# Twelve gate panels of a token mixer, given other places in TensorE's order

## The chip, the cores and the metric

The kernel runs on one core of a Trainium2 chip. The metric is the device time of one execution in microseconds (us).

## The reference, cut to what matters

Two transformer blocks on 256 tokens of width 1024, in float32. The change touches the token mixer, which is in each of the two layers of the first block:

```
proj = h @ w_in;  (a, q, k, v, qi, ki, wi, hq, hf, hi, hg, gates) = split(proj)
y_a = pool_mixer(a);  y_b = sparse_attention(q, k, v, qi, ki, wi)      # 2 blocks of 128 queries
y_c = hgrn2(hq, hf, hi, hg)                                            # gated recurrence, then
                                                                       # o * rsqrt(mean(o*o)) per head
g = sigmoid(gates.reshape(B, S, 3, D_MODEL))
merged = g[0]*(y_a @ w_branch[0]) + g[1]*(y_b @ w_branch[1]) + g[2]*(y_c @ w_branch[2])
return merged @ w_out
```

`gates` is h times 3072 columns of weights. It depends on nothing but h, and it is wanted only when the branches are merged. In attention, index scores (8 heads, ReLU, weighted sum) choose 64 keys for each query; the softmax is taken over those.

## The kernel before, in words

Weights come as panels of 1024 x 256 (1 MB) through four slots in SBUF. SP issues their DMAs in one fixed order, and waits before each until the panel four places earlier has been used. Products land in four accumulator banks `accs` that rotate in the same way; four more PSUM banks, `mix`, belong to the small products of the mixer. Each engine runs its own list, written out by hand, and waits on semaphores. All activations have tokens in the free dimension: H[:, k, lat] is 128 features by 256 tokens.

The mixer of a layer has these stages, and after each TensorE, ScalarE and VectorE wait for one another (`stage_end`): 15 input panels; pooling; attention; the recurrence; branch products (4 panels, 12 accumulators, multiplied by the gates on VectorE); output (4 panels). The 12 panels of `gates` are put between the rest: `gate(l, u)` in TensorE's list is one panel of 16 matmuls, `gate(l, u)` in ScalarE's list copies its accumulator to `gates`. Panels 0 and 1 are in pooling, 2 to 5 in attention, 6 to 11 in the recurrence.

Attention: TensorE makes the index scores of query block 0 and of block 1, then the logits of both (L812); ScalarE takes the ReLU of the scores; VectorE sums them and finds the 64 largest in 8 rounds, block 0 first, then block 1 (each round a Max8 and a MatchReplace), adds mask and bias to the logits and takes the maximum; ScalarE takes Exp; VectorE divides; TensorE transposes (L821), ScalarE copies, TensorE multiplies with v (L829), and ScalarE copies the output.

Recurrence (hgrn): 256 tokens are one tree of 8 levels. At level lv ScalarE takes the Exp of two sums, VectorE adds up the sums of the next level, multiplies (x) and takes the products of the level before out of `mix` (L1912, a copy under a mask). TensorE's products for i = 0 to 8 (L850, L853) need x of level i-1; ScalarE's Exp of level lv waits for the products i = lv-1, which read the buffer that it overwrites. Then come the output products (L861 to L863), their squares on ScalarE, mean squares over a head (L867) on TensorE, square root on ScalarE, reciprocal on VectorE, `spread` (L760, which turns the column into rows) on TensorE, and VectorE's last product. Before these, ScalarE takes the Sigmoid of all of `gates` at once.

Of the kernel before, what the change touches and what calls it, by code (L numbers as in the profile page):

```python
# [215 lines left out]
def program(nc, io):  # L216
    G, order, finished, _ = plan()
    w8, w11, wc = io["w8"], io["w11"], io["wc"]
    with ExitStack() as ctx:
# [372 lines left out]
        def _(pe):  # L592
# [203 lines left out]
            def attention(l):  # L796
                for qb in range(2):
                    n = P * (qb + 1)
                    for b in range(4):
                        if qb == 1:  # L800
                            pe.wait_ge(S("idx_relu"), 8 * l + b + 1)
                        for i in range(2):
                            r = slice(64 * (b // 2), 64 * (b // 2) + 64)
                            mm = pe.matmul(mix[:, b, i * T:i * T + n], qiT[r, 2 * (b % 2) + i, qb * P:qb * P + P], kiT[r, 0:n],
                                           start=True, stop=True)
                        mm.then_inc(S("idx_mm"), 1)
                for qb in range(2):
                    n = P * (qb + 1)
                    pe.wait_ge(S("idx_relu"), 8 * l + 4 + 2 * qb + 2)
                    for h in range(4):  # L810
                        r = slice(64 * (h % 2), 64 * (h % 2) + 64)
                        mm = pe.matmul(mix[:, 2 * qb + h % 2, h // 2 * T:h // 2 * T + n],  # L812
                                       qT[r, h // 2, qb * P:qb * P + P], kT[r, h // 2, 0:n], start=True, stop=True)
                    mm.then_inc(S("logit_mm"), 1)
                gate(l, 2, 3, 4, 5)
                for qb in range(2):
                    pe.wait_ge(S("prob_ready"), 2 * l + qb + 1)
                    for h in range(4):
                        for s in range(qb + 1):
                            i = h * (qb + 1) + s  # L820
                            mm = pe.transpose(mix[:, 2 * qb + i // 4, i % 4 * P:i % 4 * P + P],  # L821
                                              logit[:, qb, h, s * P:s * P + P], ident)
                    mm.then_inc(S("probT_mm"), 1)
                for qb in range(2):
                    pe.wait_ge(S("probT_ready"), 2 * l + qb + 1)
                    for i in range(4):
                        h = 2 * (i % 2) + i // 2
                        for s in range(qb + 1):
                            mm = pe.matmul(mix[64 * (h % 2):64 * (h % 2) + 64, 1, h // 2 * T + qb * P:h // 2 * T + qb * P + P],  # L829
                                           vt[:, s, h * 64:h * 64 + 64], probT[:, qb, i * (qb + 1) + s, :],  # L830
                                           start=(s == 0), stop=(s == qb))
                mm.then_inc(S("attn_mm"), 1)

            def hgrn(l):
                k4, q4 = kk, qf
                for i in range(9):
                    bank = 2 * (i % 2)
                    if i == 0:
# [13 lines left out]
                        for h in range(4):  # L852
                            mm = pe.matmul(mix[:, bank, h * P:h * P + P], xt[:, h, 0:P], xt[:, h, P:T], start=True, stop=True)  # L853
                    mm.then_inc(S("hg_mm"), 1)
                    if i < 6:
                        gate(l, 6 + i)
                pe.wait_ge(S("hg_acc"), 9 * l + 9)
                for h in range(4):
                    v = slice(h * P, h * P + P)
# [2 lines left out]
                    pe.matmul(o(1), hi[:, 0, v], offd[:, h, :], start=True, stop=False)  # L862
                    mm = pe.matmul(o(1), hi[:, 1, v], pairs[:, 4 + h, :], start=False, stop=True)  # L863
                mm.then_inc(S("hg_o"), 1)
                pe.wait_ge(S("hg_sq"), l + 1)
                for i in range(8):
                    mm = pe.matmul(mix[:, 0, i:i + 1], osq[:, i * P:i * P + P], ones_h[:, 0:1], start=True, stop=True)  # L867
                mm.then_inc(S("hg_ms"), 1)
                pe.wait_ge(S("hg_inverse"), l + 1)
                spread(0, 8).then_inc(S("hg_spread"), 1)  # L870

# [351 lines left out]
        def _(act):  # L1223
# [95 lines left out]
                    elif k < KD:  # L1319
                        act.drain().then_inc(S("rms_out"), 1)  # L1320

            def gate(l, *panels):
                for u in panels:
                    evac(G[f"gate{l}"], 0, u, 0, gates[:, 2 * u:2 * u + 2, :], both, ACT.Copy)

            def pool(l):
                gate(l, 0, 1)
# [4 lines left out]
            def attention(l):  # L1332
                for qb in range(2):
                    n = P * (qb + 1)
                    for pr in range(4):
                        act.wait_ge(S("idx_mm"), 8 * l + 4 * qb + pr + 1)
                        if qb == 1 and pr == 0:
                            act.wait_ge(S("idx_sum"), 2 * l + 1)
                        act.activation(relu_s[:, 2 * pr:2 * pr + 2, 0:n],
                                       mix[:, pr, :].rearrange("p (a t) -> p a t", a=2)[:, :, 0:n], ACT.Relu)\  # L1340
                           .then_inc(S("idx_relu"), 1)
                for qb in range(2):
                    n = P * (qb + 1)
                    gate(l, 2 + 2 * qb, 3 + 2 * qb)
                    act.wait_ge(S("logit_ready"), 2 * l + qb + 1)
                    for h in range(4):
                        e = act.activation(logit[:, qb, h, 0:n], logit[:, qb, h, 0:n], ACT.Exp,
                                           bias=small[:, 8 * qb + h:8 * qb + h + 1],
                                           accum_out=small[:, 8 * qb + 4 + h:8 * qb + 5 + h])
                    act.drain().then_inc(S("exp_ready"), 1)  # L1350
                for qb in range(2):
                    act.wait_ge(S("probT_mm"), 2 * l + qb + 1)
                    m = 4 * (qb + 1)
                    act.activation(probT[:, qb, 0:m, :].rearrange("p a b -> p (a b)"),
                                   mix[:, 2 * qb:2 * qb + qb + 1, :].rearrange("p a b -> p (a b)"), ACT.Copy)\
                       .then_inc(S("probT_ready"), 1)
                act.wait_ge(S("attn_mm"), l + 1)
                act.activation(ymix[:, 2:4, :].rearrange("p a b -> p (a b)"), mix[:, 1, :], ACT.Copy)

# [3 lines left out]
            def hgrn(l):  # L1363
# [3 lines left out]
                for lv in range(8):  # L1367
# [7 lines left out]
                    x = halves(treeX[lv % 2], m)  # L1375
                    act.activation(x[:, :, 0, :], halves(suff, m)[:, :, 0, :], ACT.Exp)
                    act.activation(x[:, :, 1, :], halves(pref, m)[:, :, 1, :], ACT.Exp).then_inc(S("hg_exp"), 1)
                    if lv >= 2:
                        gate(l, 4 + lv)
                act.activation(gates[:, :, :], gates[:, :, :], ACT.Sigmoid)  # L1380
                act.wait_ge(S("hg_o"), l + 1)
                act.activation(osq, mix[:, 2:4, :].rearrange("p a b -> p (a b)"), ACT.Square).then_inc(S("hg_sq"), 1)
                act.activation(rms_cols[:, 16:17], eps_rms, ACT.Sqrt)
                act.wait_ge(S("hg_ms"), l + 1)
                act.activation(rms_cols[:, 0:8], mix[:, 0, 0:8], ACT.Sqrt, bias=eps_rms).then_inc(S("hg_std"), 1)

            def gla():
                for d in range(2):
# [1212 lines left out]
```

## Time and profile before

| | us |
|---|---|
| median of 3 runs | 3429.73 (3427.65 to 3431.06) |
| profiled execution | 3429.4 |
| its span | 3427.6 |
| TensorE (PE) busy | 2980.6 (87%) |
| VectorE (DVE) busy | 1835.3 (54%) |
| ScalarE (ACT) busy | 1007.8 (29%) |
| GpSimd (POOL) busy | 192.3 (6%) |

The span is the time from the first instruction to the last. PE is TensorE's matmuls, PEld its loads of stationary weights, which lie beside them; a float32 matmul shows as two records. Times of rows are microseconds from the start of the span. Attention begins at 401.89 us in the first layer and at 1169.75 us in the second.

### The profile page before, as it was taken

The page shows a single profiled execution, that of the slowest core. Times are in us where ns is not written, and L with a number is a line of the kernel's source. Part 1 is how long each engine was busy: PE and PEld are TensorE (multiplying, and loading weights), DVE is VectorE, ACT ScalarE, POOL GpSimd, SP SyncE. Part 2 cuts the span into 40 slices and gives each one's busy share as a digit, 9 for nine tenths or more (in the row PEclk, how much of TensorE's full clock was granted, in tenths as well). Part 3 has the DMA queues.
Part 4 walks back from the last instruction along what each step waited for, and adds up shares of the span by engine and source line. Part 5 has one row for each costly group of instructions (what it writes and reads, how often), then busy time and mean ns, then how long its engine had stood idle before and what let it go on. Part 6 is the DMA issues. An engine that isn't in the chain of part 4 may idle for free.

```text
span 3427.6 us, 43953 instructions
## 1 busy us (share of the span) xinstructions
PE 2980.6 (87%) x15764; PEld 2433.0 (71%) x15764; DVE 1835.3 (54%) x3202; ACT 1007.8 (29%) x1358; POOL 192.3 (6%) x89
## 2 busy tenths in 40 slices
PE   2999988998999988888895646999999888978998
PEld 2998877998998877888784533687644454546887
DVE  5774453775767543786224762477623245452672
ACT  2431231534432131433434141333202233231211
POOL 0000000000000000000340000144100000000000
PEclk9999999999999998899897667899998999969999
DMA  7786433574666423555121001122441111102342
GB/s 280 262 302 239 167 109 123 210 267 186 263 253 237 168 99 124 196 211 195 62 74 56 1 7 49 62 99 86 176 162 50 64 59 50 43 19 86 135 165 80
DMA packets 112948, 469.03 MB, mean 137 GB/s; under 512 B 6984, under 2 KB 64912, under 8 KB 65808
## 3 DMA queue, kind: packets, MB, share of 16 engines
q1 hardware_dynamic: 112784, 466.88, 36.8%
q8 instruction: 99, 1.62, 0.2%
q14 instruction: 65, 0.53, 0.1%
HBM read 465.79 MB, written 1.06 MB: 136 GB/s over the span
## 4 chain that ended last, share of the span: by engine, by line
issue 50%; PE 37%; DVE 7%; DVEq 3%; ACT 3%; ACTq 1%; PEldq 0%; POOLq 0%; PEld 0%
PE accs L732 8%; PE accs L624 6%; PE accs L1004 4%; PE accs L637 3%; PE accs L638 3%; PE accs L639 3%; DVEq L2277 1%; ACT arena L77 1%; DVE arena L1982 1%; PE mix L1067 1%; PE mix L1044 1%; PE mix L753 1%; DVE normed L87 1%; DVE arena L87 1%; DVE arena L92 1%
## 5 line engine op out<-in xcount | busy, mean ns | idle before, releaser
L637 PE MATMUL accs<-normed_r,arena_r 128*128 128x256 f32 (+2 forms) x1864 | 594.2, 319 | 47.3 <-DVEq L1756 26.2
L638 PE MATMUL accs<-arena_r 128*128 128x256 f32 (+1 forms) x2090 | 600.6, 287 | 0.0
L624 PE MATMUL accs<-normed,panel 128*128 128x256 f32 x2432 | 541.8, 384 | 6.2 <-ACTq L1272 3.2
L624 PEld LDWEIGHTS accs<-normed,panel 128*128 128x128 f32 x2432 | 465.9, 193 | 75.7 <-issue 9.6
L637 PEld LDWEIGHTS accs<-normed_r,arena_r 128*128 128x128 f32 (+1 forms) x1864 | 358.1, 192 | 86.4 <-issue 33.6
L638 PEld LDWEIGHTS accs<-arena_r 128*128 128x128 f32 x2090 | 406.1, 194 | 1.7
L87 DVE TENSOR_TENSOR arena_r<-panel,arena_r 128x1024 fp32r<-128x1024 f32 (+1 forms) x240 | 319.7, 1332 | 149.2 <-PE accs L639 65.9
L639 PE MATMUL accs<-normed_r,arena_r 128*128 128x256 f32 x1344 | 382.2, 284 | 0.0
L1242 ACT ACTIVATE arena_r<-panel 128x1024 fp32r<-128x1024 f32 (+1 forms) x240 | 275.0, 1146 | 345.6 <-PE accs L639 213.6
L2254 DVE SCALAR_TENSOR_TENSOR arena<-accs,vectors,arena 128x189 f32<-128x189 f32 (+2 forms) x704 | 279.5, 428 | 95.9 <-issue 64.8
L1203 POOL TENSOR_TENSOR panel_r<-panel,arena_r 128x1024 fp32r<-128x1024 f32 x74 | 178.1, 2407 | 2258.3 <-ACTq L1250 2256.7
L732 PE MATMUL accs<-arena,panel 128*128 128x256 f32 (+1 forms) x960 | 285.6, 461 | 5.3 <-DVEq L431 4.7
L639 PEld LDWEIGHTS accs<-normed_r,arena_r 128*128 128x128 f32 x1344 | 259.9, 193 | 0.0
L732 PEld LDWEIGHTS accs<-arena,panel 128*128 128x128 f32 x960 | 184.1, 192 | 106.6 <-issue 84.7
L637 PE MATMUL accs<-arena_r 128*128 128x256 f32 x704 | 204.3, 290 | 21.9 <-DVEq L1756 21.9
L77 ACT ACTIVATE arena<-accs 128x512 f32<-128x512 f32 (+2 forms) x128 | 75.3, 588 | 472.6 <-PE accs L624 209.6
L92 DVE SCALAR_TENSOR_TENSOR residual<-accs,mods,residual 128x256 f32<-128x256 f32 x96 | 46.5, 484 | 298.4 <-PE accs L732 175.0
L639 PE MATMUL accs<-normed_r,panel_r 128*128 128x512 f32 (+1 forms) x520 | 205.1, 394 | 0.0
L639 PE MATMUL accs<-arena_r 128*128 128x256 f32 x704 | 201.9, 287 | 0.0
L87 DVE TENSOR_TENSOR arena<-arena 128x512 f32<-128x512 f32 (+8 forms) x216 | 142.7, 660 | 76.2 <-ACT arena L77 49.5
L1004 PE MATMUL accs<-normed,panel 128*128 128x512 f32 x384 | 178.2, 614 | 0.3 <-PEq L431 0.3
L77 ACT ACTIVATE arena<-arena 128x384 f32<-128x384 f32 (+5 forms) x136 | 100.6, 740 | 224.5 <-DVEq L2200 84.4
(285 smaller groups left out, 4075.0 us busy)
## 6 DMA issues: line engine op xcount, KB each, us to landing
panel<-w SPq DMA_DIRECT2D x250, 1024.0 KB, 4.8
panel<-w SPq DMA_DIRECT2D x48, 1408.0 KB, 8.0
cond_panel<-wc SPq DMA_DIRECT2D x60, 1024.0 KB, 5.1
normed<-wc SPq DMA_DIRECT2D x52, 1024.0 KB, 5.7
arena<-wc SPq DMA_DIRECT2D x8, 1024.0 KB, 6.5
residual<-xs SPq DMA_DIRECT2D x2, 1024.0 KB, 7.2
constants<-consts SPq DMA_DIRECT2D x1, 1152.0 KB, 8.6
residual<-crows SPq DMA_DIRECT2D x2, 512.0 KB, 7.1
```

What stands on the lines that cost most here:

```text
L77: i = self.eng.activation(*a, **k)
L87: i = self.eng.tensor_tensor(*a, **k)
L92: i = self.eng.scalar_tensor_tensor(*a, **k)
L624: mm = pe.matmul(acc[b][:, o:o + ntok], w[:, k * PANEL + j * P:k * PANEL + j * P + P], rhs(k), start=(k == 0), stop=(k == KD - 1))
L637: pe.matmul(out, hi[:, k, 0:m], src_hi(k), start=clear and k == 0, stop=False, skip_group_check=True)
L638: pe.matmul(out, hi[:, k, 0:m], src_lo(k), start=False, stop=False, skip_group_check=True)
L639: mm = pe.matmul(out, lo[:, k, 0:m], src_hi(k), start=False, stop=last and k == n - 1, skip_group_check=True)
L732: mm = pe.matmul(acc[a % BANKS][:, o:o + ntok], w[:, k * PANEL + j * P:k * PANEL + j * P + P], src(part * kper + k), start=first, stop=(pa ...
L1004: mm = pe.matmul(acc[b][:, :], w[:, k * PANEL + j * P:k * PANEL + j * P + P], H[:, k, :], start=(k == 0), stop=(k == KD - 1))
L1203: pool.tensor_tensor(lo, half_panel(g, u, j), hi, ALU.subtract)
L1242: act.eng.activation(split_parts(g, u, j)[0], half_panel(g, u, j), ACT.Copy)
L2254: dve.eng.scalar_tensor_tensor(out=out, in0=src, scalar=scale, in1=out, op0=ALU.mult, op1=ALU.add)
```

## The change

The twelve panels stay, with the same products in the same order, and move in TensorE's list. Panel 2 goes between the index scores of the two query blocks; 3, 4 and 5 stay behind the logits; 6 goes between the transposes of the two blocks; 7 ahead of the first products of the recurrence; 8 behind the products i=1 and 9 behind i=3; 10 between the output products and the mean squares; 11 between the mean squares and `spread`. ScalarE empties them in places that follow. Its one Sigmoid covers the columns of panels 0 to 9; panels 10 and 11 get theirs as they are taken from the accumulator.

```diff
--- before.py
+++ after.py
@@ -804,6 +804,8 @@
                             mm = pe.matmul(mix[:, b, i * T:i * T + n], qiT[r, 2 * (b % 2) + i, qb * P:qb * P + P], kiT[r, 0:n],
                                            start=True, stop=True)
                         mm.then_inc(S("idx_mm"), 1)
+                    if qb == 0:
+                        gate(l, 2)
                 for qb in range(2):
                     n = P * (qb + 1)
                     pe.wait_ge(S("idx_relu"), 8 * l + 4 + 2 * qb + 2)
@@ -812,7 +814,7 @@
                         mm = pe.matmul(mix[:, 2 * qb + h % 2, h // 2 * T:h // 2 * T + n],
                                        qT[r, h // 2, qb * P:qb * P + P], kT[r, h // 2, 0:n], start=True, stop=True)
                     mm.then_inc(S("logit_mm"), 1)
-                gate(l, 2, 3, 4, 5)
+                gate(l, 3, 4, 5)
                 for qb in range(2):
                     pe.wait_ge(S("prob_ready"), 2 * l + qb + 1)
                     for h in range(4):
@@ -821,6 +823,8 @@
                             mm = pe.transpose(mix[:, 2 * qb + i // 4, i % 4 * P:i % 4 * P + P],
                                               logit[:, qb, h, s * P:s * P + P], ident)
                     mm.then_inc(S("probT_mm"), 1)
+                    if qb == 0:
+                        gate(l, 6)
                 for qb in range(2):
                     pe.wait_ge(S("probT_ready"), 2 * l + qb + 1)
                     for i in range(4):
@@ -833,6 +837,7 @@
 
             def hgrn(l):
                 k4, q4 = kk, qf
+                gate(l, 7)
                 for i in range(9):
                     bank = 2 * (i % 2)
                     if i == 0:
@@ -852,8 +857,8 @@
                         for h in range(4):
                             mm = pe.matmul(mix[:, bank, h * P:h * P + P], xt[:, h, 0:P], xt[:, h, P:T], start=True, stop=True)
                     mm.then_inc(S("hg_mm"), 1)
-                    if i < 6:
-                        gate(l, 6 + i)
+                    if i in (1, 3):
+                        gate(l, 8 + i // 2)
                 pe.wait_ge(S("hg_acc"), 9 * l + 9)
                 for h in range(4):
                     v = slice(h * P, h * P + P)
@@ -862,10 +867,12 @@
                     pe.matmul(o(1), hi[:, 0, v], offd[:, h, :], start=True, stop=False)
                     mm = pe.matmul(o(1), hi[:, 1, v], pairs[:, 4 + h, :], start=False, stop=True)
                 mm.then_inc(S("hg_o"), 1)
+                gate(l, 10)
                 pe.wait_ge(S("hg_sq"), l + 1)
                 for i in range(8):
                     mm = pe.matmul(mix[:, 0, i:i + 1], osq[:, i * P:i * P + P], ones_h[:, 0:1], start=True, stop=True)
                 mm.then_inc(S("hg_ms"), 1)
+                gate(l, 11)
                 pe.wait_ge(S("hg_inverse"), l + 1)
                 spread(0, 8).then_inc(S("hg_spread"), 1)
 
@@ -1319,9 +1326,9 @@
                     elif k < KD:
                         act.drain().then_inc(S("rms_out"), 1)
 
-            def gate(l, *panels):
+            def gate(l, *panels, func=ACT.Copy):
                 for u in panels:
-                    evac(G[f"gate{l}"], 0, u, 0, gates[:, 2 * u:2 * u + 2, :], both, ACT.Copy)
+                    evac(G[f"gate{l}"], 0, u, 0, gates[:, 2 * u:2 * u + 2, :], both, func)
 
             def pool(l):
                 gate(l, 0, 1)
@@ -1335,13 +1342,14 @@
                     for pr in range(4):
                         act.wait_ge(S("idx_mm"), 8 * l + 4 * qb + pr + 1)
                         if qb == 1 and pr == 0:
+                            gate(l, 2)
                             act.wait_ge(S("idx_sum"), 2 * l + 1)
                         act.activation(relu_s[:, 2 * pr:2 * pr + 2, 0:n],
                                        mix[:, pr, :].rearrange("p (a t) -> p a t", a=2)[:, :, 0:n], ACT.Relu)\
                            .then_inc(S("idx_relu"), 1)
                 for qb in range(2):
                     n = P * (qb + 1)
-                    gate(l, 2 + 2 * qb, 3 + 2 * qb)
+                    gate(l, *((3, 4), (5,))[qb])
                     act.wait_ge(S("logit_ready"), 2 * l + qb + 1)
                     for h in range(4):
                         e = act.activation(logit[:, qb, h, 0:n], logit[:, qb, h, 0:n], ACT.Exp,
@@ -1354,6 +1362,8 @@
                     act.activation(probT[:, qb, 0:m, :].rearrange("p a b -> p (a b)"),
                                    mix[:, 2 * qb:2 * qb + qb + 1, :].rearrange("p a b -> p (a b)"), ACT.Copy)\
                        .then_inc(S("probT_ready"), 1)
+                    if qb == 0:
+                        gate(l, 6)
                 act.wait_ge(S("attn_mm"), l + 1)
                 act.activation(ymix[:, 2:4, :].rearrange("p a b -> p (a b)"), mix[:, 1, :], ACT.Copy)
 
@@ -1375,14 +1385,16 @@
                     x = halves(treeX[lv % 2], m)
                     act.activation(x[:, :, 0, :], halves(suff, m)[:, :, 0, :], ACT.Exp)
                     act.activation(x[:, :, 1, :], halves(pref, m)[:, :, 1, :], ACT.Exp).then_inc(S("hg_exp"), 1)
-                    if lv >= 2:
-                        gate(l, 4 + lv)
-                act.activation(gates[:, :, :], gates[:, :, :], ACT.Sigmoid)
+                    if lv in (1, 3, 5):
+                        gate(l, 7 + lv // 2)
+                act.activation(gates[:, 0:20, :], gates[:, 0:20, :], ACT.Sigmoid)
                 act.wait_ge(S("hg_o"), l + 1)
                 act.activation(osq, mix[:, 2:4, :].rearrange("p a b -> p (a b)"), ACT.Square).then_inc(S("hg_sq"), 1)
+                gate(l, 10, func=ACT.Sigmoid)
                 act.activation(rms_cols[:, 16:17], eps_rms, ACT.Sqrt)
                 act.wait_ge(S("hg_ms"), l + 1)
                 act.activation(rms_cols[:, 0:8], mix[:, 0, 0:8], ACT.Sqrt, bias=eps_rms).then_inc(S("hg_std"), 1)
+                gate(l, 11, func=ACT.Sigmoid)
 
             def gla():
                 for d in range(2):
```

## Rows read from the trace of the kernel before

**Rows 1.** VectorE's level take (L1912), both layers: idle before it, us, times.
```profile
  PE mix L850: 39.6, 10
```

**Rows 2.** Timeline, TensorE, recurrence: start, us, instruction xrecords, [idle before <-releaser].
```profile
454.37 3.48 PE L850 MATMUL mix<-arena 128*128 128x128 f32 x16 [3.42 <-DVEq L1898]
...
464.60 1.95 PE L850 MATMUL mix<-arena 128*128 128x128 f32 x16
466.38 7.07 PE L624 MATMUL accs<-normed,panel 128*128 128x256 f32 x32
...
515.33 0.69 PE L861 MATMUL mix<-arena 128*128 128x128 f32 x2 [1.10 <-DVEq L1916]
...
521.01 2.44 PE L867 MATMUL mix<-ones_h,arena 128*128 128x1 f32 x16 [1.11 <-ACT arena L77]
524.88 3.78 PE L760 MATMUL mix<-constants,rms_columns 128*128 128x128 f32 x16 [1.43 <-DVEq L1938]
530.06 27.89 PE L1115 MATMUL accs<-arena,panel 128*128 128x256 f32 x128 [1.40 <-ACTq L431]
```

**Rows 3.** Timeline, TensorE, attention.
```profile
401.89 4.21 PE L804 MATMUL mix<-arena 64*128 64x128 f32 x32 [1.17 <-ACTq L431]
...
409.59 2.06 PE L812 MATMUL mix<-arena 64*128 64x256 f32 x8 [0.64 <-ACT arena L77]
...
445.19 1.97 PE L821 MATMUL mix<-constants,arena 128*128 128x128 f32 x8 [4.57 <-DVE arena L87]
```

**Rows 4.** Stretches of 1 us: TensorE's busy time (records), granted clock, DMA share, GB/s.
```profile
410.00:411.00 1.00, 1.00 (x6) 0.50 0.00 0
...
413.00:414.00 1.00, 1.00 (x6) 0.97 0.02 8
...
516.00:517.00 1.00, 1.00 (x7) 0.50 0.02 8
```

**Rows 5.** Timeline, ScalarE, attention.
```profile
406.90 2.63 ACT L77 ACTIVATE arena<-mix 128x512 f32<-128x512 f32 x4 [2.43 <-DVE arena L92]
...
440.22 0.60 ACT L77 ACTIVATE arena<-accs 128x512 f32<-128x512 f32 x1 [6.31 <-PE accs L624]
440.90 0.51 ACT L77 ACTIVATE arena<-arena,small 128x256 f32<-128x256 f32 x1
...
450.99 0.60 ACT L77 ACTIVATE arena<-mix 128x512 f32<-128x512 f32 x1 [2.77 <-PE mix L829]
```

**Rows 6.** Timeline, VectorE, attention.
```profile
415.63 0.69 DVE L92 SCALAR_TENSOR_TENSOR arena<-mix,bias_causal 128x512 f32<-128x512 f32 x1
...
436.30 1.22 DVE L102 TENSOR_REDUCE small<-arena 128x4 f32<-128x1024 f32 x1
...
437.91 0.69 DVE L87 TENSOR_TENSOR arena<-arena,small 128x512 f32<-128x512 f32 x1
```

**Rows 7.** Timeline, VectorE, recurrence.
```profile
464.20 1.51 DVE L87 TENSOR_TENSOR arena<-arena 128x512 f32<-128x512 f32 x2
465.88 1.46 DVE L87 TENSOR_TENSOR arena<-arena 128x512 f32<-128x512 f32 x2 [0.17 <-issue]
467.50 1.31 DVE L1912 COPY_PREDICATED arena<-constants,mix 128x1024 f32<-128x1024 uint32 x1 [0.16 <-issue]
468.91 1.51 DVE L87 TENSOR_TENSOR arena<-arena 128x512 f32<-128x512 f32 x2
...
514.50 0.69 DVE L97 COPY arena<-mix 128x512 f32<-128x512 f32 x1
```

**Rows 8.** Timeline, ScalarE, end of the recurrence to the next stage but one.
```profile
513.48 5.32 ACT L77 ACTIVATE arena<-arena 128x6144 f32<-128x6144 f32 x1
...
521.02 1.28 ACT L77 ACT_TABLE_LOAD   x1
...
559.68 0.20 ACT L77 ACTIVATE rms_columns<-constants 128x1 f32<-128x1 f32 x1 [35.92 <-DVEq L431]
```

**Rows 9.** Page, part 6: DMA issues, KB each, median us to landing.
```profile
panel<-w SPq DMA_DIRECT2D x250, 1024.0 KB, 4.8
```

## The prediction, made before the changed kernel was run

> **What bounds the kernel now.** I read the list of engines first: TensorE is busy for 2980.6 of 3427.6 us, so it is the engine to look at, but the share says nothing of the mixer's recurrence, where each level passes from VectorE to TensorE to ScalarE and back. So I went on to the copy under predicate that takes one level's products [rows 1]: in both layers together VectorE stood idle before it 10 times, 39.6 us in all, each time for TensorE's level products (L850), although these take under 2 us. Then I read the timelines of the first layer. TensorE, once it has sent the products of a level, starts a gate panel and answers the next level only when it is through: products at 464.60, panel at 466.38 [rows 2]. Here the recurrence waits for filler. In attention it is the other way: TensorE has no panel left at 440.2 and stands still until 445.19, cold afterwards [rows 3], while VectorE and ScalarE finish the softmax. And behind the recurrence there is a chain without any filler, 515.33 to 530.06 [rows 2]. The change moves filler from the first place into the two others. I work it out in the first layer's times; the second has the same intervals, as the ten waits of [rows 1] say (five each).
>
> **Terms.** A panel is 32 records at 6.9 us at the full clock: the row at 466.38 ends at 473.45 and its predecessor's tail ends at 466.55 [rows 2]. Level products block TensorE for 1.78 us (464.60 to 466.38). A spell at the granted clock of 0.50 lasts some 3.3 us: it is at 0.50 at 410 and back at 413 [rows 4], after TensorE had stood for some 2 us. That is 1.2 GHz in place of 2.4, so a spell costs 1.65 us of work.
>
> **Attention, 401.89 to 451.69.** Panel 2 goes between the index scores of the two query blocks. Of the 4.21 us of scores the first block's, half the records at half the width, take about a third, so panel 2 runs 403.2 to 410.1, the second scores to 413.4. ScalarE has been delayed: its four Relus (2.63 us [rows 5]) start at 410.9 instead of 406.90 and end at 414.0, so the logits of block 0 are there at 413.9, those of block 1 at 415.8 (2.06 us in [rows 3], part of it cold). VectorE needs the first at 415.63 and the Relus' output at about 418 [rows 6]: cover of 1.7 us, nothing lost; without it the whole stage would slip one for one. Panels 3, 4, 5 end at 436.5, not 440.2. What held the second softmax was exactly that: ScalarE empties panel 5 at 440.22 and only then starts the Exps at 440.90, though VectorE's maximum was ready at 437.52 [rows 5, 6]. They can now start at 437.6, 3.3 us sooner, and VectorE's product ends at 441.8. But that isn't where the gain is taken: TensorE transposes block 0 once VectorE has divided it (438.60 [rows 6]), until 439.3, and then runs panel 6. After an idle stretch of 2.1 us I expect one slow spell in it: 439.3 + 6.9 + 1.65 = 447.8. Transposes of block 1 then take half their cold 1.97 us (448.8), the copy 1.05 (449.9), the output products half of the 2.77 that ScalarE waited [rows 5] (451.4), the copy 0.65: 452.1 against 451.59. **+0.5 us**, with a fifth panel done. Ends: no slow spell, -1.2; slow spell and the tail cold as before, +2.6. I take the middle one, since the row nearest (idle of 2 us ahead of 410) shows one spell and its end.
>
> **Recurrence, to the last take.** Panel 7 goes ahead of the first products. VectorE makes the key until 454.3 and the first x is only there at 462.7, a period of 4.6 before the second (465.88 + 1.46 [rows 7]); panel 7 from 451.7 is through at 458.6 (460.3 if slow), the first products by 462.1. Cost nothing; cover 0.6 us. (These are times of before; all slip by 0.5.) From there VectorE alone needs 4.71 us for a level (464.20 to 468.91 [rows 7]), of which 1.51 are sums, 1.46 x and 1.31 the take; before, with a panel in each, it was 6.9 + 1.78 = 8.7. Seven levels from 459.6, a period before 464.20, then x and takes of the last (3.7 us), would end at 496.2 in place of 515.2 (the row at 514.50 plus 0.69). Two waits are left. Panel 8 starts at 464.7 and lets the products of i=2 out at 473.4, 1.25 us after VectorE asked. Panel 9, 475.2 to 482.1, lets i=4 out at 483.9, 1.1 us late. After i=5 TensorE stands 2.9 us, so I let the last products be slow: +0.7. 496.2 + 1.25 + 1.1 + 0.75 = 499.3, with the slip 499.8. **-15.4 us** against 515.2, the slip of attention in it. Ends: 498.5 and, if panels 8 and 9 have a slow spell each, 503.1.
>
> **Behind it.** Before, 515.2 to 530.06, 14.9 us: output products 4.7, square 1.1, mean squares 2.4, root and reciprocal 1.4, spread 3.8, product 1.3. Now output products 4.7 (slow again), panel 10 6.9 (the square, 1.0 us, lies under it), mean squares 2.0 at full clock, panel 11 6.9 (the Sqrt, its table load of 1.28 us [rows 8] and the reciprocal lie under it: 2.2 of 6.9), spread 1.9 in place of a cold 3.78 [rows 2], product 1.3: 23.7. **+8.9 us.** Ends: full clock throughout, 22.0; a slow spell in both panels, 27.0. ScalarE's emptying of panel 11 needs a table load back to Sigmoid, 1.28 + 0.6, from 520.3: ready at 522.2, beside the spread, 1.2 us before VectorE's last product. ScalarE's big Sigmoid shrinks from 5.32 us to five sixths and ends ahead of the output products as before. One more load (Sqrt, for the layer norm) falls where ScalarE had stood 35.92 us [rows 8]: nothing.
> This is where the Trainium skill speaks against the change: "ScalarE: Activation LUTs" (What ACT_TABLE_LOAD costs) puts a switch of set at about 2.66 us, a load and a drain, and says to group by set. The row has a load of 1.28 us. By the page's price panel 11 would be ready at 523.6, just after VectorE's product at 523.4, and the layer would be 0.1 us dearer.
>
> **Queues.** A panel takes 4.8 us to land [rows 9]. Panel 6 may load once panel 2 is used, 410; it is wanted at 439. Branch panels 2 and 3 now wait for panels 10 and 11 (511.4, 520.3) instead of lying ready; they are wanted 14 and 21 us into the branch products, which start at 523.6. Everything that SP issues later hangs on the branch products and moves with them. Nothing.
>
> **Sum.** +0.5 of attention lies within the 15.4: -15.4 + 8.9 = -6.5 us a layer, -13 in all. The profiled execution took 3429.4 us (span 3427.6), 0.3 below the median of 3429.73: **3416.5 us**.
>
> **Rivals.**
> - *Slow spells in each moved panel.* The stretches between products are no longer filled, so the clock may fall again and again: +2.1 in attention, 1.65 in panels 8, 10 and 11: +7, a layer +0.5, so 3429 to 3431 in all, no change. For it: the three pauses over 2 us (just ahead of 409.59, of 445.19 and of 454.37 [rows 2, 3]) are each followed by half clock. Against: panels 8 and 10 come straight behind other work. The Trainium skill, "TensorE: Matmul & The Clock Gate" (HAM oscillation), describes work cut into short pieces with waits that starts cold each time; by that rule it would be this case. 0.12.
> - *No slow spell at all.* Attention -1.2, output products 3.0 and not 4.7, the last levels 0.7 sooner: 4.1 a layer more, 3408. For: less standing in total. Against: the same rows. 0.07.
> - *Cover of attention gone.* Panel 2 ends over 1.7 us late (slow spell in it) and VectorE waits for the logits: 1 to 2 us a layer back, 3419. 0.05.
> - *The tail outgrows the recurrence (slower).* Panels 10 and 11 now stand on the path in full. At 1.2 GHz they cost 27.6 in place of 13.8; from 6.5 us on, the layer is slower than before. With all of it 7.3 a layer, 3444. For: the clock is at 0.50 when the output products begin [rows 4]. Against: in its other spell of [rows 4] it was back after some 3.3 us, and the output products alone last 4.7. 0.04.
> - *It does not shorten the levels.* If ScalarE and not TensorE set 8.7 us a level, the tail alone would count: +17.8, 3447. The group [rows 1] names TensorE in all ten. 0.01.
>
> **Numbers.** Forecast 0.71, its own range 3412 to 3422. About 0.2% (6.9 us) is what a measurement can tell from no change. Faster by more takes the forecast, the second and third rival and some of the first: 0.86. Within 0.2%: 0.09. Slower: 0.05. Range 3410 to 3424: it leaves out the first and the last rivals' far ends and half of the second.
>
> **What would show it.** Right: no wait of VectorE for L850 over 1.5 us, level period near 4.7 but for i=2 and i=4; attention ends within 1 us of where it did; 23 to 24 us from the last take to the branch products. Wrong: the granted clock at 0.50 in panels 8 to 11; VectorE waiting for the logits at 415; a level period over 6 us.

## The result, and the profile after

| | us |
|---|---|
| changed kernel, median of 4 runs | 3403.13 (3402.93 to 3403.59) |
| kernel before, median of 4 runs | 3428.93 (3427.65 to 3431.06) |
| ratio | 0.9924, 95% interval 0.9907 to 0.9942 |
| profiled execution, its span | 3403.59, 3401.8 |

The change is faster by 25.8 us, 0.76%. The forecast was 3416.5 with a range of 3410 to 3424, so the gain was twice what was forecast, and the time is outside the range. A second measurement of the same kernel gave 0.9929 (0.9917 to 0.9942).

Each stage was cut at the same instructions in both traces (first index score, VectorE's first work in the recurrence, first output product, first branch product). First the kernel before, first layer; columns are length, TensorE's busy time (records), granted clock, DMA share, GB/s. A slow spell is, as in the prediction, a stretch in which the granted clock is 0.50:

```profile
401.90:451.70 49.80, 41.65 (x212) 0.90 0.28 103
451.70:515.30 63.60, 58.59 (x328) 0.97 0.29 100
515.30:530.10 14.80, 10.83 (x57) 0.65 0.00 1
```

The same three stretches of the changed kernel in the first layer, then in the second:

```profile
403.10:451.70 48.60, 45.06 (x244) 1.00 0.35 125
451.70:499.20 47.50, 39.39 (x232) 0.93 0.19 68
499.20:520.90 21.70, 20.33 (x120) 1.00 0.22 77
1161.20:1209.50 48.30, 45.09 (x245) 1.00 0.36 128
1209.50:1257.00 47.50, 39.41 (x233) 0.93 0.20 67
1257.00:1278.70 21.70, 20.30 (x121) 1.00 0.23 78
```

Attention is 1.2 us shorter with one panel more, the recurrence 16.1, the chain behind it 7.0 longer. In the chain behind the last take the granted clock rose from 0.65 to 1.00.

VectorE's wait for the level products, both layers, after the change [rows 1]:

```profile
  PE mix L855: 6.8, 6
```

39.6 us have become 6.8, and ten waits six. TensorE's timeline in attention, where [rows 3] had 445.19; times are 1.2 us late against those of the prediction, since this execution reached attention that much later:

```profile
404.71 7.17 PE L624 MATMUL accs<-normed,panel 128*128 128x256 f32 x32
...
439.85 0.66 PE L823 MATMUL mix<-constants,arena 128*128 128x128 f32 x4 [1.45 <-DVE arena L87]
440.34 7.07 PE L624 MATMUL accs<-normed,panel 128*128 128x256 f32 x32
447.25 1.04 PE L823 MATMUL mix<-constants,arena 128*128 128x128 f32 x8
...
449.40 1.58 PE L833 MATMUL mix<-arena 128*64 128x128 f32 x16 [0.52 <-ACT arena L77]
```

Eight records of transposes take 1.04 us and took 1.97; panel 6 takes 7.07 us, which is the full clock. The idle time ahead of it is 1.45 us. TensorE's timeline in the recurrence, where [rows 2] are the old ones:

```profile
464.77 7.07 PE L624 MATMUL accs<-normed,panel 128*128 128x256 f32 x32
471.68 3.73 PE L855 MATMUL mix<-arena 128*128 128x128 f32 x32
475.25 7.07 PE L624 MATMUL accs<-normed,panel 128*128 128x256 f32 x32
482.16 3.73 PE L855 MATMUL mix<-arena 128*128 128x128 f32 x32
488.84 3.10 PE L855 MATMUL mix<-arena 128*128 128x128 f32 x16 [2.94 <-DVEq L1941]
493.53 3.42 PE L855 MATMUL mix<-arena 128*128 128x128 f32 x16 [1.59 <-DVEq L1941]
...
499.22 0.49 PE L866 MATMUL mix<-arena 128*128 128x128 f32 x2 [1.37 <-DVEq L1928]
...
502.00 7.07 PE L624 MATMUL accs<-normed,panel 128*128 128x256 f32 x32
508.91 1.84 PE L873 MATMUL mix<-ones_h,arena 128*128 128x1 f32 x16
510.62 7.15 PE L624 MATMUL accs<-normed,panel 128*128 128x256 f32 x32
517.61 1.95 PE L760 MATMUL mix<-constants,rms_columns 128*128 128x128 f32 x16
520.95 27.89 PE L1122 MATMUL accs<-arena,panel 128*128 128x256 f32 x128 [1.40 <-ACTq L431]
```

Panels 8 and 9 stand where the prediction put them. The one slow spell is at i=6 and 7 (3.10 and 3.42 us in place of 1.95), where it costs little: two later traces of the same code in this place (f3_after_d6 and f2_after_d3, first layer), with 3.4 and 10.2 us at half clock there in place of 6.8, have 47.1 and 48.2 us of recurrence in place of 47.5. When the output products begin the clock is back: from 499.22 to panel 10 at 502.00 is 2.8 us, where [rows 2] had 4.6 (515.33 to 519.90). VectorE's takes of levels 2 and 4:

```profile
473.67 1.32 DVE L1924 COPY_PREDICATED arena<-constants,mix 128x1024 f32<-128x1024 uint32 x1 [1.59 <-PE mix L855]
...
484.15 1.32 DVE L1924 COPY_PREDICATED arena<-constants,mix 128x1024 f32<-128x1024 uint32 x1 [1.24 <-PE mix L855]
```

ScalarE around panel 11:

```profile
509.77 1.28 ACT L77 ACT_TABLE_LOAD   x1
511.07 0.20 ACT L77 ACTIVATE rms_columns<-constants 128x1 f32<-128x1 f32 x1
...
511.67 1.28 ACT L77 ACT_TABLE_LOAD   x1
517.81 0.60 ACT L77 ACTIVATE arena<-accs 128x512 f32<-128x512 f32 x1 [4.85 <-PE accs L624]
```

The load back to Sigmoid runs at 511.67, ahead of the wait for panel 11, not behind it.

**The sum.** Mixers of both layers: 256.5 us before (49.8 + 63.6 + 14.7, and 49.9 + 63.7 + 14.7 in the second), 235.4 after (48.6 + 47.5 + 21.7 and 48.3 + 47.5 + 21.7; the parts are rounded): -21.1. The rest of the span's 25.8 is in stages of which no instruction was changed: +2.1 ahead of and between the mixers up to the second block, -3.5 and -3.3 in two stretches of the second block. Those I call S1 (from the 6264th last matmul record to the 2464th last: even mixer, FFN, and state-space features) and S2 (from there, where the state-space groups begin, to the end). Kernel before, a second trace of it, and the changed kernel, one fence each; a second trace of the changed kernel has 1084.80 and 708.50:

```profile
1627.50:2715.70 1088.20, 902.71 (x3801) 0.87 0.20 74
2715.70:3427.60 711.90, 637.57 (x2465) 0.92 0.22 77
```
```profile
1628.60:2717.00 1088.40, 902.82 (x3802) 0.87 0.20 74
2717.00:3425.30 708.30, 623.67 (x2465) 0.94 0.22 78
```
```profile
1608.50:2693.20 1084.70, 903.47 (x3801) 0.87 0.20 74
2693.20:3401.70 708.50, 623.74 (x2465) 0.94 0.22 78
```

S2 is not the change's: a second execution of the kernel before has the short value too. The difference is one slow spell. From one and the same matmul on (the 1516th last record) the clock stayed at 0.50 for 34 us in the first trace and for 3.5 in the second:

```profile
3051.60:3085.70 34.10, 33.82 (x79) 0.50 0.00 1
```
```profile
3052.70:3056.20 3.50, 3.44 (x9) 0.52 0.00 0
```

S1 is 3.6 us longer in both traces of the one than in both of the other, and needed an experiment.

### The profile page after: what moved, and what is told of

Its sections match the earlier page's. It is cut to its first block, busy times and chain, and to the rows that moved or that the text cites. A ratio compares the mean times of both kernels' runs of the same rounds, so it can differ in the third digit from the quotient of the medians.

```text
span 3401.8 us, 43955 instructions
## 1 busy us (share of the span) xinstructions
PE 2956.8 (87%) x15764; PEld 2416.1 (71%) x15764; DVE 1834.9 (54%) x3202; ACT 1010.8 (30%) x1362; POOL 192.2 (6%) x89
## 4 chain that ended last, share of the span: by engine, by line
issue 50%; PE 36%; DVE 7%; ACT 3%; DVEq 3%; ACTq 1%; PEldq 0%; POOLq 0%; PEld 0%
PE accs L732 8%; PE accs L624 6%; PE accs L1011 4%; PE accs L637 3%; PE accs L638 3%; PE accs L639 3%; DVEq L2289 1%; ACT arena L77 1%; DVE arena L1994 1%; DVE arena L92 1%; PE mix L753 1%; DVE arena L87 1%; DVE normed L87 1%; DVE arena L82 1%; PE mix L1074 1%
## 5 line engine op out<-in xcount | busy, mean ns | idle before, releaser
L87 DVE TENSOR_TENSOR arena<-arena 128x512 f32<-128x512 f32 (+8 forms) x216 | 142.6, 660 | 74.9 <-ACT arena L77 48.2
```

The costliest lines, as they stand in the source:

```text
L87: i = self.eng.tensor_tensor(*a, **k)
```

## The experiments

My theory after the result: the panels do where they stand what the prediction's sum says, at the full clock; what the sum had too much is slow spells of TensorE's clock. The rest comes from where the second block falls against the clock's steps. The rival: something else in the change makes the unchanged stages shorter. "Mixers" is the sum of the six stretches, 256.5 us before and 235.4 after.

**e1_attention: one part alone.** The edit is against the changed kernel; `...` stands for lines left out.

```diff
-                gate(l, 7)
...
-                    if i in (1, 3):
-                        gate(l, 8 + i // 2)
+                    if i < 5:
+                        gate(l, 7 + i)
...
-                gate(l, 10)
...
-                gate(l, 11)
```

ScalarE's list follows.

> The attention part alone: panel 2 between the index scores, panel 6 between the transposes; panels 7 to 11 stand behind the recurrence's products i=0 to 4, the Sigmoid over all of the gates, nothing behind the last take. Theory (the moves work as forecast, and where the forecast fell short it was slow spells of TensorE's clock that did not come): attention ends 1.1 us sooner, and the panel missing behind i=5 frees one level, 4.1 us, so 5.2 a layer, 10.4 us in all, 3418 to 3419. Rival A (gains come from panels 10 and 11 behind the recurrence alone): no change. Rival B (5 us of the gain arise in the unchanged second block because of the clock and have nothing to do with the order of the panels): 3418 give or take 5, with the second block longer or shorter in step with its time at half clock.

Measured: 3414.11 us (7 runs, 3406.68 to 3424.96), ratio 0.9966 (0.9953 to 0.9980). Mixers 243.4, so -13.1: attention as in the changed kernel, the recurrence 3.5 shorter (4.1 expected), and the chain behind it 13.1 in place of 14.7, which nobody had expected; nothing was moved there, but its clock is 0.74 in place of 0.65. Its first layer:

```profile
403.30:452.00 48.70, 45.09 (x244) 1.00 0.35 127
452.00:512.10 60.10, 53.55 (x296) 0.94 0.24 88
512.10:525.20 13.10, 9.29 (x56) 0.74 0.00 1
```

Rival A falls: with nothing behind the last take, 13.1 of the mixers' 21.1 us are there. Rival B is not decided by it, since the runs lie 18 us apart, more than the effect, and the time is 4 us below the 3418 expected.

**e2_recurrence: the other part alone.** Panels 2 to 5 behind the logits; 6 ahead of the recurrence; 7, 8, 9 behind i=1, 3, 5; 10 and 11 as in the change. The edit is against the kernel before.

```diff
+                gate(l, 6)
...
-                    if i < 6:
-                        gate(l, 6 + i)
+                    if i in (1, 3, 5):
+                        gate(l, 7 + i // 2)
...
+                gate(l, 10)
...
+                gate(l, 11)
```

> The recurrence part alone: attention as before with panels 2 to 5 behind the logits; panel 6 ahead of the first products, 7, 8 and 9 behind i=1, 3 and 5, panels 10 and 11 behind the output products and the mean squares. Theory: levels 16 us shorter a layer (three waits for a panel in place of five, of 1.25, 1.1 and 1.05 us), the tail 7 us longer if it runs at full clock: 9 a layer, 18 in all, 3411. If the tail runs cold as the prediction had it, 8.9 longer: 14 in all, 3415.

Measured: 3407.01 us, ratio 0.9941 (0.9929 to 0.9954). The recurrence is 15.2 and 15.5 us shorter, the chain behind it 21.7 us in both layers, at the full clock: +7.0 each, so mixers -16.5, where 18 was expected. The profiled execution took 3402.37 us, the fastest of the five. The forecast's 8.9 for this chain is refused; it would have been 23.6.

**e5_fill: only the clock.** The kernel before with matmuls without use.

```diff
+            def fill(n):
+                for _ in range(n):
+                    pe.matmul(mix[:, 1, 0:T], ident, const("causal"), start=True, stop=True)
...
+                    if qb == 1:
+                        fill(9)
                     pe.wait_ge(S("prob_ready"), 2 * l + qb + 1)
...
+                        if i == 8:
+                            pe.wait_ge(S("hg_acc"), 9 * l + 7)
+                            fill(2)
...
+                fill(2)
                 pe.wait_ge(S("hg_acc"), 9 * l + 9)
+                fill(2)
                 pe.wait_ge(S("hg_sq"), l + 1)
+                fill(3)
                 pe.wait_ge(S("hg_inverse"), l + 1)
```

> The kernel before, every panel in its old place; added are matmuls without use (constants into a bank of mix that is free then), 9 in attention's gap ahead of the second transposes, 2 and 2 around i=8, 2 ahead of the mean squares and 3 ahead of the spread. They do nothing but keep TensorE's clock at full. Theory: this measures what the slow spells cost in the kernel before: transposes and output products of attention 1.8 us, output products of the recurrence 1.7, mean squares 0.5, spread 1.9, so 5 to 6 us a layer, 10 to 12 in all: 3418. Rival (the clock is a small matter): under 2 us in all, 3427 to 3430, or slower since the added matmuls stand in front of work that has become ready.

Measured: 3412.58 us, ratio 0.9964 (0.9950 to 0.9978). Mixers 245.6, -10.9, that is 5.4 a layer, of which 2.0 and 2.1 in attention, 1.5 in the recurrence, 1.9 behind it. Its first layer:

```profile
400.90:448.80 47.90, 43.11 (x230) 0.96 0.29 107
448.80:510.90 62.10, 58.86 (x336) 1.00 0.29 102
510.90:523.80 12.90, 10.68 (x66) 0.87 0.01 2
```

More work, no panel moved, and half of the change's gain in the mixers. The rival falls. So the slow spells that these matmuls took away cost the kernel before about 5.4 us a layer. That the change got the same 5.4 us by its panels is argued from this and not shown: it took away other spells, and in its chain it put longer work in their place.

**e3_no_tail: are panels 10 and 11 free behind the last take?** Against the changed kernel.

```diff
                     if i in (1, 3):
                         gate(l, 8 + i // 2)
+                    if i in (5, 6):
+                        gate(l, 5 + i)
...
-                gate(l, 10)
                 pe.wait_ge(S("hg_sq"), l + 1)
...
-                gate(l, 11)
                 pe.wait_ge(S("hg_inverse"), l + 1)
```

> The changed kernel with panels 10 and 11 taken out of the chain behind the last take and put behind the products i=5 and i=6; the Sigmoid over all of the gates. Theory: panel 10 holds the level by 1.05 us, panel 11 by another 6, so the last take comes 7 us later than in the changed kernel; the tail is 7 us shorter if it runs as cold as in the kernel before (14.9 us), 10 if at full clock. Against the changed kernel 0 to 3 us a layer sooner, so 3397 to 3404. Rival (behind the last take the panels are free, as TensorE stands there anyway): 7 us a layer slower than the changed kernel, 3417.

Measured: 3395.41 us, ratio 0.9902 (0.9884 to 0.9920). The recurrence takes 53.8 and 55.5 us, 6.3 and 8.0 more than in the changed kernel; the chain behind it 13.2 and 13.5, 8.4 less. Mixers 233.5: 1.9 less than in the changed kernel. Its first layer behind attention:

```profile
452.90:506.80 53.90, 50.28 (x297) 1.00 0.27 99
506.80:520.00 13.20, 8.41 (x57) 0.87 0.00 1
```

The rival, which had them free, falls: the panels behind the last take cost there about what they save, and this part of the change brings nothing. In the traces this kernel is 5.6 us below the changed one, and S1 alone, which nobody touched, is 6.2 less (1078.6 us). Its runs lie 22 us apart (3388 to 3410), so that its time can't be told from the changed kernel's.

**e4_one_back: panel 10 alone.** Against the changed kernel.

```diff
-                    if i in (1, 3):
+                    if i in (1, 3, 5):
                         gate(l, 8 + i // 2)
...
-                gate(l, 10)
                 pe.wait_ge(S("hg_sq"), l + 1)
```

> The changed kernel with panel 10 alone moved forward, behind the products i=5, where TensorE stands 2.9 us and then 1.6 us; panel 11 stays between the mean squares and the spread. Theory: the levels lose 1.05 us, the tail loses the panel's 6.9 and gets the wait for the squares back, 1.1: 4.7 a layer sooner than the changed kernel, 9 to 10 in all, 3394; and the slow spell that the changed kernel has at i=6 to 8 goes, up to 0.8 a layer more. Rival (the level is held for the whole panel): 0 to 2 us sooner, 3401 to 3403.

Measured: 3404.59 us, ratio 0.9928 (0.9915 to 0.9941). A miss. The recurrence loses the 1.0 us foreseen (48.5), but the chain behind it takes 20.9 and 21.2 us and not 16. Its first layer, and two rows of TensorE's timeline in the chain:

```profile
402.20:450.90 48.70, 45.09 (x244) 1.00 0.34 126
450.90:499.40 48.50, 43.66 (x265) 0.99 0.25 88
499.40:520.30 20.90, 18.39 (x89) 0.77 0.09 34
```
```profile
507.43 9.67 PE L624 MATMUL accs<-normed,panel 128*128 128x256 f32 x32
516.94 1.95 PE L760 MATMUL mix<-constants,rms_columns 128*128 128x128 f32 x16
```

Panel 11 takes 9.67 us in place of 7.1: the clock, 0.77 over the chain, took back all that the panel's better place had brought. The clock fell twice: once as the output products began, ahead of the place that the panel had left, and once in the mean squares, just behind it. In the changed kernel the slow spell lay at i=6 and 7, where it cost little; here panel 10 stands behind i=5, those products ran at full clock, and the spells came later, on the path.

**f1_best: that place, and the clock kept up.** Against e4_one_back.

```diff
+                        if i == 8:
+                            pe.wait_ge(S("hg_acc"), 9 * l + 7)
+                            fill(3)
                         pe.wait_ge(S("hg_x"), 8 * l + i)
...
+                fill(2)
                 pe.wait_ge(S("hg_acc"), 9 * l + 9)
+                fill(2)
                 pe.wait_ge(S("hg_sq"), l + 1)
```

> The changed kernel with panel 10 behind i=5 (panel 11 stays between mean squares and spread) and seven matmuls without use a layer that keep TensorE's clock up: 3 ahead of the products i=8, 2 behind them, 2 ahead of the mean squares. Theory: with panel 10 moved alone the tail ran 21 us because 10 us of it were at half clock; with the clock kept up it takes 16 to 17, the recurrence stays at 48.3, so the mixers are 4 to 5 us a layer shorter than in the changed kernel: 3394 to 3396, the second block aside, which may come out 4 us longer or 6 shorter. Rival (the tail is long for another reason, as the wait for the squares): tail 20 to 21, 3401 to 3404.

Measured: 3396.02 us, ratio 0.9915 (0.9901 to 0.9930). Its chain in the first layer:

```profile
500.10:518.10 18.00, 16.22 (x93) 0.91 0.12 38
```

It takes 18.0 us in both layers, 3 less than in e4_one_back by seven useless matmuls, so the rival (another cause for the long chain) falls; panel 11 still takes 8.84, a slow spell that the added matmuls did not keep off, so the chain is 1 to 2 us longer than expected. Mixers 229.6, 5.8 less than in the changed kernel and the shortest of all. By the whole time its interval overlaps that of the changed kernel.

**before_again and after_again.**

> The kernel before, once more, for a second trace. Theory: the first block takes the same time within 1 us in both traces, but the second block (from about 1650 us), which holds many short products with waits between, differs by up to some us in step with its time at half clock, since the moments at which the clock changes lie otherwise. Rival: the second block takes the same time to 0.5 us, and then the 5 us that it lost with the change are the change's own.

> The changed kernel once more, for a second trace. Theory: the two mixers take the same time within 1 us; the second block differs between the two traces of the changed kernel as it does between those of the kernel before, in step with its time at half clock. Rival: it is the same to 0.5 us and shorter than before in both.

Measured: 3425.57 us, ratio 0.9997 (0.9988 to 1.0006), and 3403.25 us. Mixers are the same within 0.3 us in both pairs. S2 of the kernel before changed by 3.5 us (711.9, 708.4), S1 did not. In the changed kernel neither changed, where the theory had expected S2 or S1 to. So one part of the theory held, one missed, and S1 spoke for the rival.

**f2, f3, f4, f5: the second block later.** Memsets ahead of the barrier between the blocks; f2 and f4 have three (1.4 us), f3 and f5 six (3.1 to 3.4 us by the traces), f2 and f3 on the changed kernel, f4 and f5 on the kernel before.

```diff
                         dve.wait_ge(S("x_ready"), n)
+                        for _ in range(3):
+                            dve.memset(bias_rows, 0.0)
                         stage_end(dve, count)
```

> The changed kernel; three memsets (about 1.4 us) on VectorE ahead of the barrier between the first and the second block, so that all of the second block starts that much later. Theory (where the second block lies against the moments at which TensorE's clock may change decides how long its short products take): the stretch that leads from 1650 us through the mLSTM and the FFN behind it, 1084.8 us in both traces of the changed kernel and 1088.3 in both of the kernel before, changes by more than 1 us either way, to 1088 or 1079 as in other kernels of this study, though not one instruction of it is changed. Rival (it is the change's own): it stays at 1084.8 give or take 0.3.

> As the one before with six memsets, about 2.9 us. Theory: another length than 1084.8 in this one or in the one with 1.4 us of delay, by over 1 us. Rival: 1084.8 give or take 0.3 in both.

> The kernel before with the delay of about 1.4 us ahead of the second block. Theory: the stretch that took 1088.3 us in both of its traces takes 1084.8 or less, so that the kernel is as fast as without the delay or faster, 3423 to 3428, with no panel moved. Rival: 1088.3 give or take 0.3, and 1.4 us slower.

> The kernel before with six memsets, about 2.9 us, ahead of the second block. The changed kernel with the same delay had 1092.3 and 715.0 us in the second block in place of 1084.8 and 708.5, 15 us more in all. Theory (the second block is entered in step with the clock's steps, wherever the mixers left it, and the moves of the panels are worth 21 us of mixer in any case): 1092 and 715 us here too, so 3438 to 3441, 21 us above the changed kernel with the same delay. Rival: 1088.3 and 708 to 712, as without the delay, 3430 to 3433.

| | delay | median us | ratio to before | S1 | S2 |
|---|---|---|---|---|---|
| changed | 0 | 3403.13 | 0.9924 | 1084.8 | 708.5 |
| f2 | 1.4 | 3399.24 | 0.9915 (0.9900 to 0.9930) | 1083.7 | 708.1 |
| f3 | 3.4 | 3417.95 | 0.9967 (0.9954 to 0.9980) | 1092.3 | 715.0 |
| before | 0 | 3428.93 | | 1088.3 | 711.9, 708.4 |
| f4 | 1.4 | 3423.68 | 0.9989 (0.9977 to 1.0001) | 1083.8 | 708.1 |
| f5 | 3.1 | 3435.35 | 1.0018 (1.0009 to 1.0028) | 1088.3 | 713.2 |

S1 and S2 of f3, then of f4:

```profile
1611.00:2703.30 1092.30, 911.09 (x3801) 0.86 0.20 74
2703.30:3418.30 715.00, 642.14 (x2465) 0.91 0.22 77
```
```profile
1630.20:2713.90 1083.70, 902.12 (x3801) 0.87 0.20 75
2713.90:3422.00 708.10, 622.54 (x2465) 0.95 0.22 78
```

A delay of 3.4 us makes the changed kernel 15 us slower. With one of 1.4 us its median is 4 us lower, but the intervals overlap and S1 is only 1.1 us shorter, barely the change of over 1 us that the theory had asked for. One of 1.4 us takes S1 of the kernel before from 1088.3 to 1083.8, lower than in the changed kernel. So S1 needs no moved panel to change by that much, and the rival falls. The kernel of f4 itself can't be told from the one before: its runs go from 3416 to 3432 us. f5 missed its number by 3 us, since S1 stayed at 1088.3 there, as its rival had it: I could not work out beforehand where a delay puts the block. At equal delay the changed kernel is 25.8, 24.4 and 17.4 us below the one before; its mixers were 19.6 to 21.1 us shorter each time. The cleanest pair is f2 and f4, whose S1 and S2 are the same within 0.1 us: their profiled executions are 21.1 us apart (3400.9 and 3422.0), and their mixers 20.7. That is what the moved panels are worth with the second block alike.

Is it the clock? In S2, yes by all traces: 708.5 us goes with a clock of 0.94, 715.0 with 0.91. The slow spell shown above, 3.5 us where S2 is short and 34 us where it is 711.9, lasts 47.8 us in f3 and f5 (715.0 and 713.2). In S1 only partly: f3 has the lowest, 0.86, and the longest time, but 1078.6, 1083.7 and 1088.4 all go with 0.87. There it must matter which products are slow and not how many; I did not show which. S1 in the other kernels was 1088.2 (e1), 1084.6 (e2), 1088.3 (e5), 1078.6 (e3), 1088.4 (e4) and 1084.5 us (f1), S2 between 708.4 and 708.7 in all six; e2's short S1 is one reason why its time is lower than its mixers say.

## Why the prediction was wrong

- *Attention, +0.5 a layer: wrong.* Measured -1.2 and -1.6. The failed step is "I expect one slow spell in it". The Exps did start early (439.11, 0.4 us behind VectorE's maximum and no longer 3.4), and panel 6 came when forecast. The cover held, with 1.1 us and not 1.7: the logits were there at 415.70 and VectorE took them at 416.81; but TensorE stood 1.45 us ahead of it and not 2.1, and the clock stayed at 1.00. (Whether these 0.6 us decided it was not tried.) The pause was shorter since panel 5 ended 0.7 us later than forecast. The end without a spell, -1.2, was written down and not taken. A spell could come all the same: in the first layer of e3_no_tail panel 2 took 8.86 us, VectorE waited 0.75 us for the logits, and attention took 49.2 in place of 48.6 us. That is the third rival, at 0.6 us and not the 1 to 2 that it had.
- *Recurrence: right.* With the slip taken out -15.9 was forecast, -16.1 and -16.2 measured. Waits at i=2 and i=4 of 1.25 and 1.1 us were forecast, 1.59 and 1.24 measured (the sign of being right had been no wait over 1.5); the slow spell behind i=5 came.
- *Behind the last take, +8.9: mis-sized.* Measured +7.0. The failed step is "output products 4.7 (slow again)": they took 2.8, since the spell had come earlier, at i=6 and 7, and was over. (The rows it was read from give 4.6.) Panels 10 and 11 at 7.1 us, the mean squares at 1.8 and the spread at 1.95 came as forecast.
- *Table loads: no cost.* The trace has 1.28 us and the next activation 0.02 us behind it, and neither load is on the path: the first holds the root until 511.34, while TensorE is in panel 11 until 517.6, and the second lies in a wait. The price of 2.66 us that the Trainium skill gives for a switch ("ScalarE: Activation LUTs", What ACT_TABLE_LOAD costs) does not show in these rows.
- *The sum.* For the mixers it gave -13.0, and they gave -21.1; of the 8.1 us between, attention has 3.8, the chain 3.8 and the recurrence 0.5. The rival "no slow spell at all", 3408 at a chance of 0.07, is near what the mixers did: 3429.4 - 21.1 = 3408.3. In part that is luck, since its last levels 0.7 us sooner did not come and the second layer's attention gained more than it had. The other 5 us of the miss are S1, S2 and the small changes between. The sum has no term for stages that are not changed: they were put at nothing without a reason, and the only word on them is of the queues ("Everything that SP issues later hangs on the branch products and moves with them. Nothing."). That failed too: with 3.4 us of delay S1 and S2 took 14.0 us more.
- *The rule in the first rival* (short pieces with waits start cold each time, the Trainium skill, "TensorE: Matmul & The Clock Gate", HAM oscillation) does not hold for the moved panels in the changed kernel, which ran at 1.00 in both layers, but it fits e4_one_back, where the chain with one panel less ran at 0.77 in place of 1.00.

What stays open is which products of S1 gain or lose, and what decides whether a pause brings a slow spell.

## What to carry to other kernels

Filler belongs where the engine would stand, and not where a chain waits for the engine. Where it fills a pause it can also keep TensorE's clock up for the short products behind it (5.4 us a layer here, shown by matmuls that compute nothing). Put a moved panel's price down with and without a slow spell as two forecasts, because the first decides whether a better place (e4_one_back) brings anything. And before a change of 0.5% is taken for the change's own, shift an unchanged stage by a microsecond or three and see what that does.

## What the runs showed of the hardware

In two traces of one kernel the moments at which TensorE's clock changes in S1 were the same against the work, and not against the start. Counted from one and the same matmul of S1 (the 4600th last record), the clock fell after 10.19, 61.39 and 88.70 us in one trace of the kernel before, and after 10.26, 61.46 and 88.77 in the other, although everything in that one came 1.1 to 1.3 us later. In the two traces of the changed kernel it fell after 9.58, 40.30 and 57.37, and after 9.61, 40.33 and 57.39. So S1 repeats within 0.1 us in each pair and differs between the pairs.

But such a pattern does not belong to a kernel. Different kernels share one, and then share the length of S1: in e4, e5 and f5 it fell at the same three places as in the kernel before, within 0.1 us, and S1 is 1088.3 to 1088.4 us in all; in e2 and f1 it fell at those of the changed kernel, and S1 is 1084.5 and 1084.6. f2 and f4, the two with 1.4 us of delay, share a third pattern, with 1083.7 and 1083.8. (Three moments do not fix the length by themselves: in e1 and f3 the clock fell after 10.2, 40.9 and 61.4 us, and S1 is 1088.2 and 1092.3.) And one kernel can have several: the kernel before had S2 at 711.9 us and at 708.4, and in one series its 13 executions took 3419.7 to 3435.1 us, the fastest at a mean granted clock of 0.923 and the slowest at 0.917. So a change in one place can draw another pattern for what follows, a delay alone can do it, and sometimes nothing does but another execution.

The slow spell of 34 us in S2 came although TensorE was busy in 33.8 of its 34.1 us by the records; at the full clock the same engine was busy only in part of the time there (19.6 of the 30.6 us from 3056.2 on, in the second trace).
